# Expert pairs on one core: scatter products of 64 rows for each column half, the pass branch of VectorE ahead of the last pair, and repeated products on TensorE inside the last pair

## The chip, the core and the metric

The kernel runs on one core of a Trainium2 chip. The core has a matrix engine (PE, TensorE), a vector engine (DVE), a scalar engine (ACT), GpSimd (POOL) and a queue engine (SP), which here only issues transfers. Each engine has an instruction stream of its own, and they wait for each other through semaphores. The metric is the device time of one execution in microseconds (us).

## The reference, cut to what matters

A two-layer encoder on 256 tokens of width 1024, all in float32. Each layer has a dense part (convolution, attention, cross attention) and then a mixture of 32 experts, of which each token uses two. The change lies in the expert part.

```
def hier_moe(u, w_group, b_group, w_router, b_router, w1, w3, w2):
    ...
    weights = g_w * jax.nn.softmax(top_v, axis=-1)
    expert = (g_sel * EXPERTS_PER_GROUP + top_i).astype(jnp.int32)
    y = grouped_swiglu(xf, expert, w1, w3, w2)
    out = jnp.einsum('nkd,nk->nd', y, weights.astype(y.dtype))
    return out.reshape(B, S, D)

def expert_block(args):              # inside grouped_swiglu
    xb, e = args
    hdn = jax.nn.silu(xb @ w1[e]) * (xb @ w3[e])
    return hdn @ w2[e]

def reference(...):
    for i in range(DEPTH):           # DEPTH = 2
        ...
        h = h + hier_moe(rmsnorm(h, norm_ffn_g[i]), ...)
    return rmsnorm(h, final_norm_g)
```

## The kernel before, in words

The 32 experts of a layer are worked through as 16 pairs. A pass gives each expert up to 32 tokens (CAP); if some expert has more, all pairs are gone through again, which these inputs do not ask for. For one pair PE runs these steps, each in a function of its own:

- `gather`: multiplies the token rows by a 0/1 selection (`sel`, made by DVE), so that the tokens of the pair's two experts lie side by side.
- `up_product` (L2132): tokens times w1 and w3 of both experts. For each of 8 chunks there are four products, 32 columns of the array each, so the four share the array. Its first half waits for the semaphores of the first halves of the weights, its second half for those of the second halves.
- `turn_up` (L2150): four transposes of the result, once ACT has copied it out of PSUM (L1102). ACT then takes silu (L1106) and DVE multiplies (L1612).
- `down_product` (L2161): the hidden columns times w2. Its four products give, for expert e and column half h of the output, 32 rows of PSUM bank 3 at block 2e + h.
- `turn_spread` (L2113): transposes `spread`, the selection times the router's weight (DVE, L1597), written twice (`dup`) so that each of the four 32-row blocks has a copy. ACT copies it out as `scat` in two versions (L1087, L1088), one with the rows of column half 1 zeroed by a mask column of the constants, one with those of half 0 zeroed.
- `scatter` (L2173): after DVE has copied bank 3 to `y_sb` (L1616), four products of 128 rows (two token halves s, two column halves) add the pair's result to the residual rows, which stand in PSUM banks 4 to 7. After each s it raises the semaphore `added[s]`.

SP brings in the weights, 12.6 MB a pair, into slots that PE frees through the semaphore `freed`. The slabs of the last pair of a layer come in halves. In layer 0 the first slabs of layer 1's dense part (w_xkv, then w_in) are queued behind them.

Around the last pair: PE, DVE, ACT and SP each run the middle pairs in a loop. PE then loads the number of passes from SBUF (L2216), branches (L2217) over a block that holds all pairs once more, and does `last_pair` behind it (L2200). DVE does the last two pairs' part (`pair_tail`) behind its loop, and only then loads the number and branches (L1652, L1653). After the last layer ACT squares the summed rows (L1127), DVE scales them (L1673 to L1678) and SP stores them. After layer 0 the next dense part begins: ACT splits landed weights in a high part (L819) and DVE in a low part (L1213), DVE splits the memory operand (L1278), and PE runs its products high (L1753, L1754) and low (L1758).

The order of all work on an engine is the order in which the code is written. `again` (L2081 on) repeats a product of two constants into a PSUM bank that nobody reads; the kernel before calls it around the router.

## Time and profile before

| | us |
|---|---|
| median of 3 timed runs | 1727.71 |
| lowest and highest of them | 1727.01, 1729.36 |
| the profiled execution | 1730.33 |
| its span in the trace | 1728.5 |
| PE busy, share of the span | 1485.5, 86% |
| DVE busy | 616.5, 36% |
| ACT busy | 521.4, 30% |
| mean granted PE clock, of full speed | 0.928 |

The profile is of one execution. Busy shares are averages over parts with different limits: in the dense parts PE is busy without a gap and the transfer engines are partly idle, in the expert parts it is the other way round. A row of the timeline gives the start in us from the span's start, the duration in us, the engine, the source line, the operation, the tiles, and the count; brackets give the idle time before it and what ended it. "PEldq" and "DVEq" are the sequencers of PE and DVE, which run registers, loads and branches.

### The profile page before, as it was taken

To read this page: it belongs to the slowest core of one execution; us is meant where nothing else is said; L and a number is where in the kernel's file an instruction comes from. 1 tells how busy PE (TensorE), PEld (TensorE's weight loads), DVE (VectorE), ACT (ScalarE), POOL (GpSimd) and SP (SyncE) were. 2 spreads that over 40 slices of the span, in tenths; PEclk is the share of its full clock that TensorE was granted. 3 is DMA by queue.
4 is the path that set the end of the run, shared out by engine and by line. 5 is a ranking of instruction groups with operands and counts; after the bars stand their busy time and mean duration, and the time that the engine had idled before them with its cause. 6 is when DMAs were issued, how large, how long until landed. Compare 5 with 4: busy or idle time off the path is not lost.

```text
span 1728.5 us, 23513 instructions
## 1 busy us (share of the span) xinstructions
PE 1485.5 (86%) x9704; PEld 992.7 (57%) x9704; DVE 616.5 (36%) x1020; ACT 521.4 (30%) x825; POOL 49.5 (3%) x96
## 2 busy tenths in 40 slices
PE   8999999999976767676799999999999676867676
PEld 7879889897432323232277888998864232323222
DVE  5557786654110000001064668775531000000101
ACT  5535655553100000000163465635431000000001
POOL 3011000000000000000000200000000000000000
PEclk8999999999998888888899999999999888888888
DMA  8536344766999999999964462357579999999997
GB/s 236 195 122 212 106 147 162 276 243 266 385 426 428 429 427 428 428 428 429 418 220 169 129 206 99 136 206 286 201 304 429 427 428 428 429 427 430 428 426 289
DMA packets 92832, 531.08 MB, mean 307 GB/s; under 512 B 5992, under 2 KB 6184, under 8 KB 66118
## 3 DMA queue, kind: packets, MB, share of 16 engines
q1 hardware_dynamic: 89600, 524.12, 75.6%
q0 software_dynamic: 3136, 5.73, 1.6%
q8 instruction: 61, 1.00, 0.2%
q14 instruction: 23, 0.19, 0.0%
q10 hardware_dynamic: 12, 0.05, 0.0%
HBM read 524.63 MB, written 1.05 MB: 304 GB/s over the span
## 4 chain that ended last, share of the span: by engine, by line
PE 65%; DMA 30%; DVE 2%; ACT 2%; issue 1%; PEldq 0%; DVEq 0%; SPq 0%; ACTq 0%
DMA ring<-in_w_dram 28%; PE ps L2132 16%; PE ps L1753 7%; PE ps L1758 7%; PE ps L1754 7%; PE ps L1809 4%; PE ps L1810 4%; PE ps L1815 4%; PE ps L2104 2%; DMA ring<-in_w_xkv_dram 2%; PE ps L1855 2%; PE ps L2161 2%; PE ps L1778 1%; PE ps L1784 1%; PE ps L1779 1%; PE ps L2173 1%
## 5 line engine op out<-in xcount | busy, mean ns | idle before, releaser
L2132 PE MATMUL ps<-ring,work 128*32 128x512 f32 x1440 | 282.4, 720 | 190.1 <-DMA ring<-in_w_dram 182.5
L1213 DVE TENSOR_TENSOR weight_split<-ring,weight_split 128x1024 fp32r<-128x1024 f32 x224 | 270.7, 1222 | 163.4 <-ACT weight_split L819 161.3
L819 ACT ACTIVATE weight_split<-ring 128x1024 fp32r<-128x1024 f32 x224 | 234.2, 1058 | 216.0 <-PE ps L1815 86.0
L2132 PEld LDWEIGHTS ps<-ring,work 128*32 128x32 f32 x1440 | 69.2, 130 | 389.7 <-DMA ring<-in_w_dram 203.3
L1612 DVE TENSOR_TENSOR work<-tail,ps 128x256 f32<-128x256 f32 x32 | 13.5, 421 | 661.2 <-ACT tail L1106 661.2
L1753 PE MATMUL ps<-operand_split,weight_split 128*128 128x256 f32 x896 | 227.7, 292 | 1.2 <-PE ps L1758 0.6
L1754 PE MATMUL ps<-operand_split,weight_split 128*128 128x256 f32 x896 | 219.5, 282 | 0.0
L2132 PE MATMUL ps<-big,work 128*32 128x512 f32 x576 | 192.6, 705 | 1.1 <-DVE work L1604 1.1
L1753 PEld LDWEIGHTS ps<-operand_split,weight_split 128*128 128x128 f32 x896 | 171.0, 191 | 15.0 <-issue 12.9
L1754 PEld LDWEIGHTS ps<-operand_split,weight_split 128*128 128x128 f32 x896 | 171.3, 191 | 2.0 <-issue 1.9
L1102 ACT ACTIVATE tail<-ps 128x512 f32<-128x512 f32 x32 | 33.7, 1054 | 443.7 <-PE ps L2132 443.7
L2104 PEld LDWEIGHTS ps<-work,big 128*128 128x128 f32 x1024 | 119.1, 192 | 38.4 <-issue 37.0
L2104 PE MATMUL ps<-work,big 128*128 128x64 f32 x1024 | 124.2, 275 | 9.9 <-PE ps L2132 9.9
L1758 PE MATMUL ps<-operand_split,weight_split 128*128 128x256 f32 x896 | 125.8, 283 | 0.6 <-DVE weight_split L1213 0.6
L2173 PE MATMUL ps<-sqo,tail 128*128 128x512 f32 x256 | 118.4, 605 | 3.2 <-DVE sqo L1616 1.6
L1758 PEld LDWEIGHTS ps<-operand_split,weight_split 128*128 128x128 f32 x896 | 115.6, 192 | 0.8 <-DVE weight_split L1213 0.8
L1809 PE MATMUL ps<-weight_split,operand_split 128*128 128x512 f32 x288 | 114.4, 397 | 0.0
L1810 PE MATMUL ps<-weight_split,operand_split 128*128 128x512 f32 x288 | 113.3, 393 | 0.0
L1087 ACT ACTIVATE tail<-ps,cst 128x256 f32<-128x256 f32 x32 | 15.2, 474 | 301.2 <-PE ps L2173 287.1
L2161 PE MATMUL ps<-ring,work 128*32 128x512 f32 x544 | 81.8, 602 | 0.0
L2173 PEld LDWEIGHTS ps<-sqo,tail 128*128 128x128 f32 x256 | 46.0, 189 | 58.1 <-issue 45.9
L1815 PE MATMUL ps<-weight_split,operand_split 128*128 128x512 f32 x288 | 77.8, 392 | 0.0
(253 smaller groups left out, 1692.5 us busy)
## 6 DMA issues: line engine op xcount, KB each, us to landing
ring<-in_w_dram SPq DMA_DIRECT2D x118, 2048.0 KB, 28.4
big<-in_w_dram SPq DMA_DIRECT2D x56, 2048.0 KB, 27.2
ring<-in_w_in_dram SPq DMA_DIRECT2D x28, 2048.0 KB, 8.0
big<-in_w_dram SPq DMA_DIRECT2D x20, 1024.0 KB, 18.8
ring<-in_w_xkv_dram SPq DMA_DIRECT2D x8, 2048.0 KB, 8.1
ring<-in_w_dram SPq DMA_DIRECT2D x12, 1024.0 KB, 22.4
ring<-in_w_attn_out_dram SPq DMA_DIRECT2D x4, 2048.0 KB, 7.9
ring<-in_w_conv_out_dram SPq DMA_DIRECT2D x4, 2048.0 KB, 8.4
```

The costliest lines, as they stand in the source:

```text
L819: act.activation(split_quarter(k, 0), landed_quarter(k), ACT.Copy).then_inc(w_hi, 1)
L1213: dve.tensor_tensor(split_quarter(k, 1), landed_quarter(k), split_quarter(k, 0).bitcast(F32), ALU.subtract).then_inc(w_lo, 1)
L1753: pe.matmul(dst, hi[:, k, :], xs[0][:, k, :], start=(k == 0), stop=False)
L1754: pe.matmul(dst, hi[:, k, :], xs[1][:, k, :], start=False, stop=False)
L1758: last = pe.matmul(dst, lo[:, k, :], xs[0][:, k, :], start=False, stop=(k == DC - 1))
L1809: pe.matmul(dst[s], xh, hi[:, k, :], start=(c == 0 and k == 0), stop=False)
L1810: pe.matmul(dst[s], xl, hi[:, k, :], start=False, stop=False)
L1815: last = pe.matmul(dst[s], xs[0][:, 2 * c + k, s * P:(s + 1) * P], lo[:, k, :], start=False, stop=False)
L2104: last = pe.matmul(ps[:, 0, c * 2 * CAP:(c + 1) * 2 * CAP], uN[:, s, c * P:(c + 1) * P], sel[:, s].rearrange("p e s -> p (e s)"), start=(s ...
L2132: last = pe.matmul(ps[CAP * j:CAP * (j + 1), 1, :], xe[:, k, e * CAP:(e + 1) * CAP], up_slot(slots[j])[:, k, :], start=(k == 0), stop=(k = ...
L2161: last = pe.matmul(ps[CAP * j:CAP * (j + 1), 3, :], up_t[:, f, e, :], down_slot(slots[4 + e])[:, f, half * SLAB:(half + 1) * SLAB], start= ...
L2173: last = pe.matmul(ps[:, 4 + 2 * s + half, :], scat[:, half, s * P:(s + 1) * P], y_sb, start=False, stop=True, skip_group_check=True)
```

## The change

Four things are changed.

1. Scatter. `down_product` puts expert e and column half h at block 2h + e, so that one column half fills 64 neighbouring rows. `spread` is laid out to match. ACT makes one plain copy `scat` in place of two masked ones, and each of the four scatter products takes the 64 rows of its column half in place of 128 rows half of which are zero. The mask constants go, and `scat` has half its size.
2. DVE. The load of the number of passes and the branch stand ahead of the last pair's `pair_tail` in place of behind it.
3. PE, last pair only. `up_product` calls `again(5, 0)` behind its wait for the tokens and ahead of its wait for the weights.
4. PE, last pair only. `again(1, 0)` stands between `up_product` and `turn_up`, and again between `turn_up` and `down_product`.

```
...
-C_MLO = C_SIGN + 1
-C_MHI = C_MLO + 1
-C_LAM = C_MHI + 1
+C_LAM = C_SIGN + 1
...
+WARM_UP = 5
...
-    c[:, C_MLO] = (p // CAP) % 2 == 0
-    c[:, C_MHI] = (p // CAP) % 2 == 1
...
-        tail = sb("tail", [P, 2 * T + SLAB + FC * 2 * CAP])
+        tail = sb("tail", [P, T + SLAB + FC * 2 * CAP])
...
-        scat = rt(2, T)
+        scat = rt(T)
...
                 def scatter_columns(n):
                     act.wait_ge(gt_done, n + 1)
-                    act.activation(scat[:, 0, :], ps[:, 2, 0:T], ACT.Copy, scale=cst[:, C_MLO:C_MLO + 1])
-                    act.activation(scat[:, 1, :], ps[:, 2, 0:T], ACT.Copy,
-                                   scale=cst[:, C_MHI:C_MHI + 1]).then_inc(scat_ready, 1)
+                    act.activation(scat, ps[:, 2, 0:T], ACT.Copy).then_inc(scat_ready, 1)
                 def next_scatter_columns():
...
                     if again:
                         dve.wait_ge(gt_done, n)
                     for dup in range(2):
-                        dve.tensor_tensor(spread[:, :, :, dup, :], sel,
+                        dve.tensor_tensor(spread[:, :, dup, :, :], sel,
                                           two(tok_w, i).unsqueeze(3).to_broadcast([P, TT, 2, CAP]),
                                           ALU.mult).then_inc(spread_ready, 1)
...
                 with dve.Fori(0, PAIRS - 2) as i:
                     pair_two_on(i)
                 pair_tail(dve.snap(u))
-                pair_tail(dve.snap(u), more=False)
                 passes = dve.value_load(npass_i[0:1, 0:1], min_val=1, max_val=MAX_PASSES)
                 with dve.If(passes > 1):
                     with dve.Fori(1, passes) as _p:
+                        pair_tail(dve.snap(u), more=False)
                         dve.drain()
                         dve.tensor_scalar(rank, rank, -float(CAP), None, ALU.add)
                         dve.drain()
...
                         with dve.Fori(0, PAIRS - 2) as i:
                             pair_two_on(i)
                         pair_tail(dve.snap(u))
-                        pair_tail(dve.snap(u), more=False)
                     dve.nop()
-                dve.nop()
+                pair_tail(dve.snap(u), more=False)
             fc = Chain(dve, fin_ch)
             dve.wait_ge(fin_g, 16)
...
                     pe.wait_ge(spread_ready, n * 2 + 2)
                     for s in range(TT):
                         last = pe.transpose(ps[:, 2, s * P:(s + 1) * P],
-                                            spread[:, s].rearrange("p e w s -> p (e w s)"), ident)
+                                            spread[:, s].rearrange("p w e s -> p (w e s)"), ident)
                     last.then_inc(gt_done, 1)
                 def first_tokens():
...
                     gather(n, 1)
                     turn_spread(n)
-                def up_product(n, slots, landed):
+                def up_product(n, slots, landed, more):
                     pe.wait_ge(xe_ready, n + 1)
+                    if not more:
+                        again(WARM_UP, 0)
                     for k in range(DC):
                         if k % (DC // 2) == 0:
                             pe.wait_ge(*landed[k // (DC // 2)])
...
                             pe.wait_ge(*landed[f // 2])
                         for j in range(4):
                             e, half = j // 2, j % 2
-                            last = pe.matmul(ps[CAP * j:CAP * (j + 1), 3, :], up_t[:, f, e, :],
+                            g = 2 * half + e
+                            last = pe.matmul(ps[CAP * g:CAP * (g + 1), 3, :], up_t[:, f, e, :],
                                              down_slot(slots[4 + e])[:, f, half * SLAB:(half + 1) * SLAB], start=(f == 0),
                                              stop=(f == FC - 1), skip_group_check=True)
                     last.then_inc(y_done, 1)
...
                     pe.wait_ge(y_out, n + 1)
                     for s in range(TT):
                         for half in range(HALVES):
-                            last = pe.matmul(ps[:, 4 + 2 * s + half, :], scat[:, half, s * P:(s + 1) * P], y_sb,
+                            at = slice(2 * CAP * half, 2 * CAP * (half + 1))
+                            last = pe.matmul(ps[:, 4 + 2 * s + half, :], scat[at, s * P:(s + 1) * P], y_sb[at, :],
                                              start=False, stop=True, skip_group_check=True)
                         last.then_inc(added[s], 1)
                     pe.reg_add(u, u, 1)
...
                 def pair(slots, ups, downs, more=True):
                     n = pe.snap(u)
-                    up_product(n, slots, ups)
+                    up_product(n, slots, ups, more)
                     if more:
                         gather(n + 1, 0)
+                    else:
+                        again(1, 0)
                     turn_up(n)
                     if more:
                         gather(n + 1, 1)
+                    else:
+                        again(1, 0)
                     down_product(n, slots, downs)
                     if more:
                         turn_spread(n + 1)
```

PE at the end of the program, from the last pair's first row on, before. `ring` and `big` are weight slots, `work` the tokens, `cst` the constants, `tail` the copied result:

```order
L2200 ISA
L2129 ISA [waits moe_tokens_ready]
L2132 MATMUL ps<-ring,work 32x512 [waits last_up_halves_0_landed]
...
L2150 MATMUL ps<-cst,tail 128x128 [waits moe_up_done,moe_scatter_ready,moe_up_out]
L2150 MATMUL ps<-cst,tail 128x128 x3
L2158 ISA [waits moe_hidden_ready]
L2161 MATMUL ps<-big,work 32x512 [waits last_down_halves_0_landed]
```

The same place now:

```order
L2202 ISA
L2078 MATMUL ps<-cst 128x512 [waits moe_tokens_ready]
L2078 MATMUL ps<-cst 128x512 x4
L2125 ISA
L2128 MATMUL ps<-ring,work 32x512 [waits last_up_halves_0_landed]
...
L2078 MATMUL ps<-cst 128x512 [waits moe_up_done]
L2146 MATMUL ps<-cst,tail 128x128 [waits moe_scatter_ready,moe_up_out]
L2146 MATMUL ps<-cst,tail 128x128 x3
L2078 MATMUL ps<-cst 128x512
L2154 ISA [waits moe_hidden_ready]
L2158 MATMUL ps<-big,work 32x512 [waits last_down_halves_0_landed]
```

Five products of 512 columns stand between the branch and the last pair's first weight product, and one before and one behind the transposes; all stand behind the branch.

DVE at the end of the program, before, from the end of the block that is branched over:

```order
L1612 TENSOR_TENSOR work<-tail,ps 128x256 [waits moe_silu_ready]
L1616 COPY sqo<-ps 128x512 [waits moe_down_done]
L1617 ISA
L1654 COMPARE_AND_BRANCH
L1653 UNCONDITIONAL_BRANCH
L1673 TENSOR_SCALAR small<-small 128x1 [waits final_squares,final_gain_in]
```

And now:

```order
L1612 ISA
L1648 COMPARE_AND_BRANCH
L1647 UNCONDITIONAL_BRANCH
L1660 ISA
L1607 TENSOR_TENSOR work<-tail,ps 128x256 [waits moe_silu_ready]
L1611 COPY sqo<-ps 128x512 [waits moe_down_done]
L1667 TENSOR_SCALAR small<-small 128x1 [waits final_squares,final_gain_in]
```

The last pair's multiply and copy have moved behind the branch; what follows them is the next work without a branch between.

## Rows read from the trace of the kernel before

**Rows 1.** Busy time of a stretch: length, PE, PEld, DVE, ACT, POOL; granted clock, DMA share, GB/s.

```profile
480.00:830.00 350.00, 250.66 (x1680) 105.53 (x1680) 29.92 (x72) 27.33 (x48) 0.00 (x0) 0.85 1.01 428
```

**Rows 2.** The chain that ended last, layer 1's last pair: start us, us, what.

```profile
1699.91 10.07 PE ps L2132 x64
...
1712.76 5.34 PE ps L2161 x32
...
1718.87 2.00 PE ps L2173 x4
```

**Rows 3.** PE's sequencer by line: ns min/median/max, first and last start us.

```profile
L2216 PEldq TENSOR_LOAD <-npass_i x2: 314/403/492, 842.3 to 1692.8; - x2
...
L2217 PEldq COMPARE_BRANCH  x2: 6152/6164/6176, 843.2 to 1693.5; - x2
```

**Rows 4.** The same for the branches of PE's loop and of DVE's pass branch.

```profile
L2211 PEldq COMPARE_BRANCH  x8: 76/213/252, 576.9 to 1692.7; - x8
...
L1653 DVEq COMPARE_BRANCH  x2: 56/62/67, 867.5 to 1718.9; - x2
```

**Rows 5.** Transfers in 846 to 848 us, the instruction queue: packets, MB, share.

```profile
q8 instruction: 1, 0.02, 3.4%
```

**Rows 6.** Timeline of SP: issues of layer 1's last pair, two of them.

```profile
1680.38 0.80 SPq L568 DMA_DIRECT2D ring<-in_w_dram  x2
...
1683.81 0.33 SPq L568 DMA_DIRECT2D ring<-in_w_dram  x1
```

**Rows 7.** Issue to landing, us at the end: first issued at 1680.38, then at 1683.81.

```profile
ring<-in_w_dram SPq DMA_DIRECT2D x1, 1024.0 KB, 14.0
...
ring<-in_w_dram SPq DMA_DIRECT2D x1, 1024.0 KB, 20.4
```

**Rows 8.** Timeline of PE around layer 0's last pair.

```profile
842.08 3.70 PE L2173 MATMUL ps<-sqo,tail 128*128 128x512 f32 x8
849.65 1.05 PE L2132 MATMUL ps<-ring,work 128*32 128x512 f32 x1 [3.88 <-issue]
...
861.24 0.62 PE L2161 MATMUL ps<-big,work 128*32 128x512 f32 x2 [1.00 <-DVE work L1612]
...
864.56 0.62 PE L2161 MATMUL ps<-big,work 128*32 128x512 f32 x2 [1.40 <-DMA ring<-in_w_dram]
...
867.30 3.70 PE L2173 MATMUL ps<-sqo,tail 128*128 128x512 f32 x8 [0.81 <-DVE sqo L1616]
871.08 0.38 PE L1753 MATMUL ps<-operand_split,weight_split 128*128 128x256 f32 x1
```

**Rows 9.** Stretches of both last pairs, columns as in rows 1.

```profile
849.65:852.50 2.85, 2.85 (x16) 0.81 (x20) 0.00 (x0) 0.00 (x0) 0.00 (x0) 0.50 1.03 428
...
1699.91:1705.90 5.99, 5.99 (x30) 1.44 (x34) 0.00 (x0) 0.00 (x0) 0.00 (x0) 0.50 1.00 414
...
1712.76:1716.10 3.34, 3.34 (x16) 0.81 (x20) 0.00 (x0) 0.92 (x2) 0.00 (x0) 0.50 0.08 32
```

**Rows 10.** Pieces of the chain in layer 1 at the full clock.

```profile
1276.60 1.72 PE ps L2084 x4
...
1296.24 3.62 PE ps L2161 x32
...
1304.33 7.05 PE ps L2132 x64
```

**Rows 11.** Timeline of ACT behind layer 0's last pair.

```profile
869.97 2.01 ACT L819 ACTIVATE weight_split<-ring 128x1024 fp32r<-128x1024 f32 x2 [4.61 <-DMA ring<-in_w_xkv_dram]
```

**Rows 12.** Timeline of DVE behind layer 0's last pair.

```profile
867.76 3.25 DVE L1278 SCALAR_TENSOR_TENSOR operand_split<-memT,pk,operand_split 128x256 fp32r<-128x256 f32 x8 [0.52 <-issue]
871.06 1.23 DVE L1213 TENSOR_TENSOR weight_split<-ring,weight_split 128x1024 fp32r<-128x1024 f32 x1
```

**Rows 13.** The chain that ended last, behind layer 0: PE's first low products.

```profile
873.25 0.96 PE ps L1758 x8
```

**Rows 14.** Groups by line, 871 to 1260 us, PE: busy, mean ns, idle before.

```profile
L1753 PE MATMUL ps<-operand_split,weight_split 128*128 128x256 f32 x448 | 113.4, 291 | 0.4 <-PE ps L1758 0.3
```

More of the change, by code:

```diff
@@ L59 @@
 C_SIGN = C_INVF + 1
-C_MLO = C_SIGN + 1
-C_MHI = C_MLO + 1
-C_LAM = C_MHI + 1
+C_LAM = C_SIGN + 1
 C_OML = C_LAM + LAYERS
@@ L97 @@
 UPS = 2 * UP_HALF
+WARM_UP = 5
 PER_PAIR = UPS + 4
@@ L235, in constants @@
     c[:, C_INVF] = np.exp(step * (p % HALF).astype(np.float32) / np.float32(HALF))
-    c[:, C_MLO] = (p // CAP) % 2 == 0
-    c[:, C_MHI] = (p // CAP) % 2 == 1
     for i in range(LAYERS):
@@ L271, in encoder @@
         sqo = sb("sqo", [P, ATTN_STEPS // 4, P])
-        tail = sb("tail", [P, 2 * T + SLAB + FC * 2 * CAP])
+        tail = sb("tail", [P, T + SLAB + FC * 2 * CAP])
         ps = ctx.enter_context(nc.psum_tensor("ps", [P, 8, SLAB], F32))
@@ L407, in encoder @@
         roff[0] = 0
-        scat = rt(2, T)
+        scat = rt(T)
         up_sb = rt(SLAB)
@@ L1086, in scatter_columns @@
                     act.wait_ge(gt_done, n + 1)
-                    act.activation(scat[:, 0, :], ps[:, 2, 0:T], ACT.Copy, scale=cst[:, C_MLO:C_MLO + 1])
-                    act.activation(scat[:, 1, :], ps[:, 2, 0:T], ACT.Copy,
-                                   scale=cst[:, C_MHI:C_MHI + 1]).then_inc(scat_ready, 1)
+                    act.activation(scat, ps[:, 2, 0:T], ACT.Copy).then_inc(scat_ready, 1)
                 def next_scatter_columns():
@@ L1596, in pair_spread @@
                     for dup in range(2):
-                        dve.tensor_tensor(spread[:, :, :, dup, :], sel,
+                        dve.tensor_tensor(spread[:, :, dup, :, :], sel,
                                           two(tok_w, i).unsqueeze(3).to_broadcast([P, TT, 2, CAP]),
@@ L1650, in _ @@
                 pair_tail(dve.snap(u))
-                pair_tail(dve.snap(u), more=False)
                 passes = dve.value_load(npass_i[0:1, 0:1], min_val=1, max_val=MAX_PASSES)
@@ L1654, in _ @@
                     with dve.Fori(1, passes) as _p:
+                        pair_tail(dve.snap(u), more=False)
                         dve.drain()
@@ L1663, in _ @@
                         pair_tail(dve.snap(u))
-                        pair_tail(dve.snap(u), more=False)
                     dve.nop()
-                dve.nop()
+                pair_tail(dve.snap(u), more=False)
             fc = Chain(dve, fin_ch)
@@ L2113, in turn_spread @@
                         last = pe.transpose(ps[:, 2, s * P:(s + 1) * P],
-                                            spread[:, s].rearrange("p e w s -> p (e w s)"), ident)
+                                            spread[:, s].rearrange("p w e s -> p (w e s)"), ident)
                     last.then_inc(gt_done, 1)
@@ L2122, in first_tokens, with up_product @@
                     turn_spread(n)
-                def up_product(n, slots, landed):
+                def up_product(n, slots, landed, more):
                     pe.wait_ge(xe_ready, n + 1)
+                    if not more:
+                        again(WARM_UP, 0)
                     for k in range(DC):
@@ L2160, in down_product @@
                             e, half = j // 2, j % 2
-                            last = pe.matmul(ps[CAP * j:CAP * (j + 1), 3, :], up_t[:, f, e, :],
+                            g = 2 * half + e
+                            last = pe.matmul(ps[CAP * g:CAP * (g + 1), 3, :], up_t[:, f, e, :],
                                              down_slot(slots[4 + e])[:, f, half * SLAB:(half + 1) * SLAB], start=(f == 0),
@@ L2172, in scatter @@
                         for half in range(HALVES):
-                            last = pe.matmul(ps[:, 4 + 2 * s + half, :], scat[:, half, s * P:(s + 1) * P], y_sb,
+                            at = slice(2 * CAP * half, 2 * CAP * (half + 1))
+                            last = pe.matmul(ps[:, 4 + 2 * s + half, :], scat[at, s * P:(s + 1) * P], y_sb[at, :],
                                              start=False, stop=True, skip_group_check=True)
@@ L2180, in pair @@
                     n = pe.snap(u)
-                    up_product(n, slots, ups)
+                    up_product(n, slots, ups, more)
                     if more:
                         gather(n + 1, 0)
+                    else:
+                        again(1, 0)
                     turn_up(n)
@@ L2186, in pair @@
                         gather(n + 1, 1)
+                    else:
+                        again(1, 0)
                     down_product(n, slots, downs)
```

## The prediction

> **What bounds the kernel now.** I read the stretches first. From 480 to 830 us, inside layer 0's expert part, the transfer engines are full (428 GB/s, share 1.01) while PE is busy for 250.66 of 350 us [rows 1]: each pair waits for its weights. Whatever PE, DVE or ACT save in those pairs is therefore saved in idle time. This goes for the shorter scatter of pairs 0 to 14, for the one ACT copy in place of two, and for the `spread` layout; I cost all three at nothing, and the cover is those 99 us of idle PE time, about 8 us a pair.
>
> So the change can only show where the transfers run out: at the last pair of each layer. There I read the chain of waits. In layer 1 the last pair's up product begins at 1699.91 and takes 10.07, the down product begins at 1712.76 and takes 5.34, the scatter begins at 1718.87, and its first half is over after 2.00 [rows 2]. Layer 0 is read from the timeline: up product at 849.65, down product at 861.24 with a wait for a transfer until 864.56, scatter at 867.30 [rows 8].
>
> **Why PE waits before the last pair.** The change treats this wait as one that may be filled, so what ends it decides. PE idles 3.88 us before 849.65, and the profile names no releaser ("issue") [rows 8]. The weights are not it: the last of the first halves is issued at 1680.38 and lands 14.0 us later, at 1694.4, 5.5 us before PE begins [rows 6, 7]. What fits is PE's own sequencer: it loads the number of passes at 842.3 and 1692.8, begins the branch at 843.2 and 1693.5, and this branch takes 6.15 and 6.18 us, so it ends at 849.4 and 1699.7, when the product begins [rows 3]. A loop branch on the same sequencer takes at most 0.25 us, DVE's pass branch at most 0.07 [rows 4]. One packet of the instruction queue moves between 846 and 848 [rows 5], so I read the stall as a fetch of the code branched to. All added products stand behind this branch, so they begin where the wait ends.
>
> The Trainium skill ("Runtime: NRT & Kernel Launch", Instruction fetch mechanics) says that a taken branch whose target is outside of the pages at hand has to fetch them before it can go on. The rows agree: 6.16 us and one instruction packet. By that rule the stall does not depend on what PE still computes, which speaks against the first rival below.
>
> **The change part by part.** The sum is made against the profiled execution (1730.33, span 1728.5), which is 2.6 above the median of 1727.71; I then add the difference to the median.
>
> *Five repeated products.* Four records of a repeated product, two products, take 1.72 at the full clock, so one is 0.86 and five are 4.28 [rows 10]. After the stall the clock is low, at 0.50 of full, which is the 1.2 of its two levels of 1.2 and 2.4 GHz: from 849.65 for 2.85 us in layer 0, and from 1699.91 for 5.99 us in layer 1 [rows 9]. A low clock costs half of its duration, now as before; only other work is done in it. So the up product ends 4.28 later than now in layer 1. In layer 0 it ended at 861.24 less the chain of 2.77 between the two products, at 858.47. Now: 849.65 + 4.28 + 7.05 at full clock [rows 10] + half of 2.85 = 862.4, 3.9 later.
>
> *One product on either side of the transposes.* 0.86 each. From the end of the up product to the down product 2.77 us pass (1712.76 less 1709.98 in layer 1) [rows 2], of which the transposes take some 0.6, the rest being waits for ACT and DVE; before the down product PE idles 1.00 [rows 8]. Both fit at full clock and cost nothing; at the low clock (1.7 each) each would add some 0.7. I take nothing, as the five products ahead have by then raised the clock.
>
> *Down product.* In layer 1 it takes 5.34 because the clock fell once more, to 0.50 from 1712.76 to 1716.1, after PE had stood idle for most of the 2.8 us before [rows 2, 9]; at full clock it takes 3.62 [rows 10]. With PE fed in between, I expect the fall to go: 1.7 saved. In layer 0 it had not fallen. So the timed runs may have had this loss or not, and the saving in them is 0 to 1.7.
>
> *Scatter.* Eight records take 3.70 [rows 8]. No product on 64 rows is in the trace. The nearest row is the up product: four tiles of 32 columns share the array, so 64 records take 7.05, 0.44 for each four [rows 10]. If two tiles of 64 rows share it likewise, the scatter takes half: 1.9. If not, 3.70 as now. I take 1.9, by the column tiles. At the end of the program this is worth 0.9: the first square starts that much sooner, and ACT does the second one only behind the first one's root, so the rest moves along.
>
> *DVE's branch.* In layer 0 DVE pauses 0.52 between its copy and L1278 [rows 12]. Ahead of the last pair DVE has no work during the whole up product (10.07 in layer 1 [rows 2]); that hides the branch, and 0.5 goes from DVE behind layer 0. In layer 1 DVE waits for ACT's square at that point, so nothing is gained.
>
> *Layer 1's end, summed:* + 4.28 - 0.9 - (1.7 or 0) = + 1.7 or + 3.4.
>
> *Layer 0's end.* Here the transfer at 864.56 hides work today, and behind the pair PE waits for ACT's first split, whose slab lands at 869.97 [rows 11]. Now the down product begins at 862.4 + 2.77 = 865.2, has its weights, and ends at 868.8 instead of 866.5. DVE copies 0.69, then does its eight L1278 in 3.25 and the first L1213 in 1.23 [rows 12]: 868.8 + 0.7 + 0.1 + 3.25 + 1.23 = 874.1, against 872.3 today. PE's scatter ends at 871.5, its high products (1.9 us) at 873.4, and it then has to wait for that L1213. Its first low products stood at about 873.0 to 873.1 in the trace (873.25 in the chain [rows 13]) and now start at 874.15: + 1.1. In the dense part that follows PE has next to no gap (the 448 products of L1753 found it idle for 0.4 us in all [rows 14]), so this stays. Had the low clock lasted 5.99 instead of 2.85, as in layer 1, it would be + 2.6. The transfers at 864.56 hid that difference before; they no longer do.
>
> *Together:* 1.7 + 1.1 = + 2.8 at the least, 3.4 + 2.6 = + 6.0 at the most. The one layer shows the short low clock, the other the long one, so I take the middle: + 4.3, that is 1727.7 + 4.3 = 1732.0.
>
> **The rivals.** *First, the other side: the stall hangs on the scatter.* The fetched packet moves about 1 us behind the end of the scatter of pair 14 (842.08 + 3.70 = 845.8), and in both layers that distance is alike. If the branch is held until PE has drained, the scatter's 1.8 us come off the start of the last pair. Then layer 1 gives -0.1 to + 1.6 and layer 0, which falls back under the cover of the transfers, 0 to + 0.8: together -0.1 to + 2.4, around 1728.8. Against it: loop branches take 0.25 us at most while the same scatters run [rows 4]. It turns the verdict to "no change" if more than about 1 us of the scatter's gain reaches the start.
>
> *Second, the 64-row products do not share the array.* The scatter stays at 3.70. Layer 1 loses its 0.9; in layer 0 PE is held by its own scatter until 873.3, 2.2 behind today, 3.7 with the long low clock. Together + 4.8 to + 8.0, around 1734.1. The Trainium skill ("TensorEngine Tiling (Array Packing)", Key Properties) says that tiles operate independently and may run in parallel; no product on 64 rows is in this trace.
>
> *Third, the wait is one that can be filled.* If the repeated products ran inside the wait, say because the stall shortens as the code moves by 16 rows, the up product would run at full clock and be held only by the second halves, which land at 1683.81 + 20.4 = 1704.2 [rows 6, 7]. It would end at 1704.2 + 3.5 = 1707.7 instead of 1710.0, and the down product would begin at 1710.5. Its last weights land between 1712.8, as the transfer share is 0.08 from there on, and some 1.4 later [rows 9], so with 1.8 for its second half it ends between 1714.6 and 1716.0 instead of 1718.1. With the scatter's 0.9, and nothing in layer 0, that is -3.0 to -4.4, around 1724.0. Against it: the added code stands behind the branch, and the stall is the same 6.16 in both layers.
>
> **Chances.** A measurement of this kernel can tell about 0.2%, 3.5 us, from no change; that is 1731.2. Forecast 0.61, of which three quarters lie above 1731.2 (its span is 1730.5 to 1733.7). First rival 0.18, all within. Second 0.11, all above. Third 0.07, half of it beyond -3.5. 0.03 for what I don't see. Slower: 0.46 + 0.11 + 0.01 = 0.58. Same: 0.15 + 0.18 + 0.03 + 0.01 = 0.37. Faster: 0.04 + 0.01 = 0.05. The range runs from 1727.8 (leaving out the third rival and the lower half of the first) to 1734.5 (leaving out the upper part of the second).
>
> **What would show it.** In the profile of the changed kernel: PE's pass branch again at about 6.16 us, beginning 1 us after the scatter of pair 14 begins, and ten records of the repeated product behind it, the first at about 849.6; if the branch ends 1.8 sooner relative to that scatter's start, the first rival is right. The eight scatter records in 1.9 or in 3.7. The up product of layer 1 ending near 1714.2, of layer 0 near 862.4. No clock of 0.50 in the down products. In layer 0 the row of the transfer ending PE's wait gone, DVE's first L1213 at about 872.9, and PE's first L1758 about 1.1 to 2.6 later than 873.1. The forecast is wrong if the repeated products begin before the branch ends, or if the branch is far from 6.16 us.

## The result, and the profile after

| | before | changed |
|---|---|---|
| median of 20 runs each, alternating, us | 1727.01 | 1732.2 |
| lowest and highest | 1724.64, 1730.08 | 1728.34, 1735.77 |
| the profiled execution | 1730.33 | 1733.08 |
| its span | 1728.5 | 1731.3 |

The ratio is 1.0026, with a 95% interval of 1.002 to 1.0033: 4.5 us slower, between 3.5 and 5.7; the medians are 5.2 apart. The page of the changed kernel:

```profile
span 1731.3 us, 23538 instructions
...
PE 1439.4 (83%) x9732; PEld 974.7 (56%) x9732; DVE 616.5 (36%) x1020; ACT 506.7 (29%) x793; POOL 49.4 (3%) x96
```

PE is busy for 46 us less than before and ACT for 15 us less, and the kernel is slower. Nearly all of that saving fell in pairs that wait for their weights. The stretch of [rows 1], now:

```profile
480.00:830.00 350.00, 227.45 (x1672) 94.77 (x1674) 29.97 (x72) 20.82 (x35) 0.00 (x0) 0.83 1.01 428
```

Half of PE's saving, 23.2 us, lies in this stretch, and the transfers run at the same 428 GB/s.

PE's pass branch, by line (ns min/median/max, first and last start us):

```profile
L2219 PEldq COMPARE_BRANCH  x2: 6077/6124/6172, 842.8 to 1696.0; - x2
```

The last pair of layer 1 in the chain that ended last (start us, us, what):

```profile
1695.01 1.99 PE ps L2171 x8
1697.00 5.20 issue
1702.20 5.96 PE ps L2078 x10
1708.16 7.05 PE ps L2128 x64
...
1718.00 3.68 PE ps L2158 x32
...
1722.45 1.15 PE ps L2171 x4
```

L2171 is the scatter, L2078 a repeated product, L2128 the up product, L2158 the down product. The scatter's eight records take 1.99, against 3.70 [rows 8], but the "issue" behind it has grown to 5.20. In the chain of the kernel before it was:

```profile
1696.23 3.68 issue
```

The branch begins 1.0 to 1.2 us behind the start of the scatter, as before, and lasts as long as before [rows 3]. One packet of the instruction queue moves 3 to 4 us behind its start, in 1699 to 1700 us, as one did 3 to 5 us behind it before [rows 5]:

```profile
q8 instruction: 1, 0.02, 6.7%
```

Then come the ten records of the five products, and only then the up product. Beside rows 2: the repeated and up products take 13.01 where the up product took 10.07, the down product 3.68 where it took 5.34, and the first half of the last scatter 1.15 where it took 2.00.

Layer 0, PE's timeline:

```profile
849.10 7.54 PE L2078 MATMUL ps<-cst 128*128 128x512 f32 x10 [5.50 <-issue]
...
863.82 1.10 PE L2078 MATMUL ps<-cst 128*128 128x512 f32 x2 [0.18 <-PE ps L2128]
864.82 0.66 PE L2146 MATMUL ps<-cst,tail 128*128 128x128 f32 x4
865.31 1.02 PE L2078 MATMUL ps<-cst 128*128 128x512 f32 x2
866.48 0.62 PE L2158 MATMUL ps<-big,work 128*32 128x512 f32 x2
...
870.93 1.99 PE L2171 MATMUL ps<-sqo,tail 64*128 64x512 f32 x8 [0.81 <-DVE sqo L1611]
...
875.23 0.98 PE L1752 MATMUL ps<-operand_split,weight_split 128*128 128x256 f32 x6 [0.21 <-DVE weight_split L1208]
```

The row of a transfer that ended PE's wait at 864.56 [rows 8] has no counterpart: the up product now ends past 863, and the down product starts late with all its weights there. What PE then waits for, at 875.23, is DVE's low part of the first weights. The first low products stood at about 873.1 before (873.25 in the chain [rows 13]). DVE's timeline shows the chain that leads there, and that its branch's pause of 0.52 [rows 12] is gone:

```profile
870.18 0.69 DVE L1611 COPY sqo<-ps 128x512 f32<-128x512 f32 x1 [3.84 <-PE ps L2158]
870.79 3.25 DVE L1273 SCALAR_TENSOR_TENSOR operand_split<-memT,pk,operand_split 128x256 fp32r<-128x256 f32 x8
...
873.96 1.22 DVE L1208 TENSOR_TENSOR weight_split<-ring,weight_split 128x1024 fp32r<-128x1024 f32 x1
```

The mean granted clock, as a share of full speed, in three stretches: the repeated products of layer 0, those of layer 1, and layer 1's down product (columns as in rows 1, the clock third from the end).

```profile
849.10:856.60 7.50, 7.50 (x14) 2.90 (x15) 0.00 (x0) 0.00 (x0) 0.00 (x0) 0.60 1.01 419
...
1702.20:1708.16 5.96, 5.96 (x14) 2.46 (x18) 0.00 (x0) 0.00 (x0) 0.00 (x0) 0.76 1.01 418
...
1718.00:1721.70 3.70, 3.64 (x32) 0.97 (x32) 0.00 (x0) 0.92 (x2) 0.00 (x0) 1.00 0.00 0
```

From the means, at 0.50 and 1.00 of full, the low clock (1.2 GHz) lasted 6.0 us in layer 0 (7.50 x (1 - 0.60) / 0.5) and 2.9 us in layer 1. Before it was 2.85 and 5.99 [rows 9]: the same two lengths, in the other order.

### The profile page after: what moved, and what is told of

Its sections match the earlier page's. It is cut to its first block, busy times and chain, and to the rows that moved or that the text cites. A ratio compares the mean times of both kernels' runs of the same rounds, so it can differ in the third digit from the quotient of the medians.

```text
span 1731.3 us, 23538 instructions
## 1 busy us (share of the span) xinstructions
PE 1439.4 (83%) x9732; PEld 974.7 (56%) x9732; DVE 616.5 (36%) x1020; ACT 506.7 (29%) x793; POOL 49.4 (3%) x96
## 4 chain that ended last, share of the span: by engine, by line
PE 63%; DMA 31%; DVE 3%; ACT 1%; issue 1%; PEldq 0%; SPq 0%; DVEq 0%; ACTq 0%
DMA ring<-in_w_dram 30%; PE ps L2128 15%; PE ps L1747 7%; PE ps L1752 7%; PE ps L1748 7%; PE ps L1803 4%; PE ps L1804 4%; PE ps L1809 4%; PE ps L1849 2%; PE ps L2098 1%; PE ps L1772 1%; PE ps L1778 1%; PE ps L2158 1%; PE ps L1773 1%; PE ps L2078 1%
## 5 line engine op out<-in xcount | busy, mean ns | idle before, releaser
L2128 PE MATMUL ps<-ring,work 128*32 128x512 f32 x1440 | 275.6, 708 | 231.6 <-DMA ring<-in_w_dram 231.6
L1208 DVE TENSOR_TENSOR weight_split<-ring,weight_split 128x1024 fp32r<-128x1024 f32 x224 | 270.4, 1223 | 159.8 <-ACT weight_split L816 157.8
L2128 PEld LDWEIGHTS ps<-ring,work 128*32 128x32 f32 x1440 | 68.1, 128 | 425.5 <-DMA ring<-in_w_dram 253.2
L2128 PE MATMUL ps<-big,work 128*32 128x512 f32 x576 | 187.1, 684 | 1.1 <-DVE work L1599 1.1
L2098 PE MATMUL ps<-work,big 128*128 128x64 f32 x1024 | 124.2, 275 | 10.1 <-PE ps L2128 10.1
L1084 ACT ACTIVATE tail<-ps 128x256 f32<-128x256 f32 x32 | 12.3, 384 | 250.0 <-PE ps L2171 236.0
L2158 PE MATMUL ps<-ring,work 128*32 128x512 f32 x544 | 80.0, 595 | 0.0
L2158 PE MATMUL ps<-big,work 128*32 128x512 f32 x480 | 72.7, 595 | 0.3
L2171 PE MATMUL ps<-sqo,tail 64*128 64x512 f32 x256 | 63.6, 615 | 3.2 <-DVE sqo L1611 1.6
```

What stands on the lines that cost most here:

```text
L1208: dve.tensor_tensor(split_quarter(k, 1), landed_quarter(k), split_quarter(k, 0).bitcast(F32), ALU.subtract).then_inc(w_lo, 1)
L2098: last = pe.matmul(ps[:, 0, c * 2 * CAP:(c + 1) * 2 * CAP], uN[:, s, c * P:(c + 1) * P], sel[:, s].rearrange("p e s -> p (e s)"), start=(s ...
L2128: last = pe.matmul(ps[CAP * j:CAP * (j + 1), 1, :], xe[:, k, e * CAP:(e + 1) * CAP], up_slot(slots[j])[:, k, :], start=(k == 0), stop=(k = ...
L2158: last = pe.matmul(ps[CAP * g:CAP * (g + 1), 3, :], up_t[:, f, e, :], down_slot(slots[4 + e])[:, f, half * SLAB:(half + 1) * SLAB], start= ...
L2171: last = pe.matmul(ps[:, 4 + 2 * s + half, :], scat[at, s * P:(s + 1) * P], y_sb[at, :], start=False, stop=True, skip_group_check=True)
```

## The experiments

The theory: the whole loss is the five repeated products, because they stand behind PE's pass branch and so begin only when it ends. The rivals were those of the prediction; after the first runs the question was what the wait itself costs. Each run has one profile. Runs 1 to 4 shared one chip and one set of runs of the kernel before (median 1727.18), runs 5 to 8 another (1726.82), runs 9 and 10 a third (1726.92). Ratios are against these.

**1. Only the five products, on the kernel before.** (`...` marks what is left out of an edit.)

```
...
-                def up_product(n, slots, landed):
+                def up_product(n, slots, landed, more):
                     pe.wait_ge(xe_ready, n + 1)
+                    if not more:
+                        again(WARM_UP, 0)
```

> The kernel before with the five repeated products alone, everything else as before. My theory (the products begin only when PE's pass branch has ended, with the weights landed, so they push the last pair out): + 4.3 at layer 1's end, less 1.7 if the clock stays up in the down product, and in layer 0 PE's scatter, still 3.70 us long, ends 2.2 to 3.7 later; together + 4.8 to + 8.0 against before. Rival (the wait is one that can be filled, the products run inside it): 0 or below, -3 at best. In the profile: ten records of the repeated product behind the branch, which takes 6.1 to 6.2 us.

Measured: 1733.17, ratio 1.0037 (1.0023 to 1.005), that is 6.4 us slower (4.0 to 8.6). Its chain:

```profile
1695.72 3.70 PE ps L2176 x8
1699.42 3.60 issue
1703.01 6.04 PE ps L2085 x10
1709.06 7.05 PE ps L2135 x64
...
1718.88 5.38 PE ps L2164 x32
```

The 3.60 of idle time is about what it was before (3.68), and the ten records stand behind it. Note the last row: the down product again takes 5.38, at a mean clock of 0.68. So in layer 1 the five products did not keep the clock up across the gap behind the up product; in layer 0 of this profile it stayed at 1.00.

**2. The changed kernel without the five.**

```
                     pe.wait_ge(xe_ready, n + 1)
-                    if not more:
-                        again(WARM_UP, 0)
```

> The changed kernel without the five repeated products; the scatter of 64 rows, DVE's earlier branch and the two single products stay. My theory: all of the loss goes. Layer 1 gains 0.9 from the scatter and 0 to 1.7 from the clock in the down product, layer 0 is covered by its transfers again: -0.9 to -2.6 against before. Rival (the loss comes from another part, from the 64-row scatter or the moved branch): still + 3 or more against before. In the profile: first up product of the last pair at 7.2 to 7.4 us behind the start of the scatter ahead.

Measured: 1725.24, ratio 0.9984 (0.9975 to 0.9993), 2.8 us faster than before (1.2 to 4.3), the lowest ratio of all the kernels here.

```profile
1694.82 1.99 PE ps L2169 x8
...
1702.23 10.01 PE ps L2126 x64
...
1715.03 3.68 PE ps L2156 x32
...
1719.48 1.15 PE ps L2169 x4
```

The up product takes 10.01 as before, while down product and scatter have the short times of the changed kernel. So the other parts of the change are worth 2.8, and the five products cost 7.3 on top of them (1.0026 less 0.9984, times 1727; by the two intervals some 5 to 9).

**3. The single products gone too.**

```
                     if more:
                         gather(n + 1, 0)
-                    else:
-                        again(1, 0)
                     turn_up(n)
                     if more:
                         gather(n + 1, 1)
-                    else:
-                        again(1, 0)
```

> The changed kernel without any repeated product in the last pair. It differs from the run without the five by the two single products alone. My theory: -0.9 against before, with the down product of layer 1 at the low clock in some executions; so 0 to 1.7 slower than the run without the five. Rival (the single products lie on the path and cost 0.1 to 0.2 each in both layers): faster than that run by 0.2 to 0.4.

Measured: 1725.66, ratio 0.9994 (0.9985 to 1.0003). By the ratios this is 1.7 slower than run 2, by the medians 0.4, and the intervals overlap. It fits the expectation without proving it. In its one profile, an execution of 1722.86, layer 1's down product ran at the full clock without any single product (first row, its first half), and its second half was then held by its last weights; layer 0's ran at a mean of 0.69 (second row; columns as in rows 1):

```profile
1706.47:1708.37 1.90, 1.90 (x16) 0.42 (x16) 0.00 (x0) 0.92 (x2) 0.00 (x0) 1.00 0.72 302
858.52:863.70 5.18, 5.18 (x32) 1.18 (x32) 0.00 (x0) 4.11 (x10) 0.00 (x0) 0.69 1.05 388
```

So the fall of the clock ahead of the down product comes in some executions and layers and not in others. Over all profiles, two layers each: without the single products (before and runs 1, 3, 5, 8, 10) 8 of 12 down products ran at a mean clock of 0.67 to 0.70; with them (changed and runs 2, 4, 6, 7, 9) all 12 ran at 1.00.

**4. Ten products in place of five.**

```
-WARM_UP = 5
+WARM_UP = 10
```

> The changed kernel with ten in place of five repeated products. My theory: each product is 0.86 us of PE on the path in both layers, at full clock by then: + 4.3 in layer 1 and + 4.3 in layer 0, where nothing covers them any more, so + 8.6 against the changed kernel and + 12.5 to + 14 against before. Rival (part of the five still lies in a wait, so they cost less than the next five): the difference to the changed kernel is clearly more than twice that kernel's loss plus what the scatter gives back; by the profile the first five cost 4.3 less covers, so the slope tells. Rival (the price is the low clock and not the work): less than + 4 against the changed kernel.

Measured: 1740.33, ratio 1.0083 (1.0069 to 1.0097): 8.1 above the changed kernel by the medians, 9.8 by the ratios. Five more products a layer, ten in all, at 0.86 make 8.6.

```profile
1701.69 10.26 PE ps L2078 x20
1711.95 7.05 PE ps L2128 x64
```

By this slope each further product behind the branch costs its own length. Five had already used up what cover there was, layer 0's transfer at 864.56 [rows 8].

**5. The branch three pairs earlier, on the kernel before.** If the branch's 6 us stall is what costs, it should pay to put it where PE waits for weights anyway.

```
-                with pe.Fori(1, TRIPLES) as _i:
+                with pe.Fori(1, TRIPLES - 1) as _i:
                     for kind in range(KINDS):
                         kind_pair(kind)
...
                 passes = pe.value_load(npass_i[0:1, 0:1], min_val=1, max_val=MAX_PASSES)
                 with pe.If(passes > 1):
...
+                for kind in range(KINDS):
+                    kind_pair(kind)
                 last_pair()
```

> The kernel before with PE's load of the passes and its branch three pairs earlier: the loop runs one round less, and the last round stands behind the branch. Theory (the wait ahead of the last pair is the fetch behind the branch, and the branch can hide where PE waits for weights anyway): the idle time of 3.7 to 3.9 us ahead of the last pair goes, the up product follows the scatter at once and then waits for its second halves, which land at about 1704.2; layer 1 ends 1 to 3 us sooner, layer 0 is held by its transfers at 864.56 as before; together -1 to -3. Rival (the wait is one for weights): the idle time stays and nothing changes. In the profile the branch of 6.2 us lies ahead of pair 12, where PE idles more than 8 us anyway.

Measured: 1728.99, ratio 1.0011 (0.9998 to 1.0023). Not faster; the expectation was wrong. The stall has moved:

```profile
L2217 PEldq COMPARE_BRANCH  x2: 6399/6548/6697, 751.9 to 1603.8; - x2
```

But a wait for the second halves of the weights has taken its place in layer 1:

```profile
1683.36 20.03 DMA ring<-in_w_dram
...
1703.43 6.56 PE ps L2132 x32
...
1712.77 5.31 PE ps L2161 x32
```

PE starts the up product early, stops between its halves until 1703.4, and does the second half in 6.56 at the low clock, where 3.5 was to be had. It ends at 1709.99; before, it ended at 1709.98 [rows 2], in a span of the same 1728.5. In layer 0 its timeline shows such a wait too, of 3.65 us:

```profile
852.46 1.05 PE L2132 MATMUL ps<-ring,work 128*32 128x512 f32 x1 [3.65 <-DMA ring<-in_w_dram]
```

**6. The same on run 2's kernel** (the edit of run 5 without `again(5, 0)`).

> The changed kernel without the five repeated products, and with PE's branch three pairs earlier. Theory: what the run without the five gives and what the earlier branch gives, partly the same microseconds, since the transfers become the bound: -2 to -4.2 against before.

Measured: 1725.59, ratio 0.9996 (0.9987 to 1.0005). The -2 to -4.2 expected did not come, and nothing was gained over run 2 (0.9984).

```profile
1679.31 21.07 DMA ring<-in_w_dram
...
1700.42 5.55 PE ps L2126 x32
```

The second half starts when its transfer lands and runs partly at the low clock.

Moving the branch also tests what the stall is. In run 5 a packet of the instruction queue moves 3 to 5 us behind the start of the branch in both layers, as before and after the change, though the branch stands some 90 us earlier; the kernel before moves no such packet in 749 to 760 or in 1600 to 1615. That fits a fetch of the code branched to. It is no proof: run 5 also moves one between 841 and 850, where PE has no such stall.

**7. Run 6 with the five products between the halves of the up product.** Here the wait is one for data, so it can be filled. (Shown against run 6.)

```
                     for k in range(DC):
+                        if k == DC // 2 and not more:
+                            again(WARM_UP, 0)
                         if k % (DC // 2) == 0:
                             pe.wait_ge(*landed[k // (DC // 2)])
```

> The same with the five repeated products put between the two halves of the last pair's up product, where PE now waits for the second halves. Theory: they lie inside a real wait here (some 6 us in layer 1), cost nothing, and keep the clock up for the second half: -3 to -4.2 against before, 0 to 1.5 faster than the run without them. Rival (repeated products always cost): slower than that run by 2 or more.

Measured: 1726.05, ratio 0.9997 (0.9987 to 1.0006). The same five products that cost some 7 us behind the branch cost nothing that can be told here (0.5 us by the medians against run 6, 0.2 by the ratios, within either interval). PE's timeline of layer 0:

```profile
846.64 4.56 PE L2078 MATMUL ps<-cst 128*128 128x512 f32 x10
...
852.88 0.62 PE L2128 MATMUL ps<-ring,work 128*32 128x512 f32 x1 [1.68 <-DMA ring<-in_w_dram]
```

They run at full clock, and 1.68 us of the wait are left behind them (1.79 in layer 1). But they gain nothing either, and the -3 to -4.2 expected failed: in layer 1 the last transfer of the program now ends the chain.

```profile
1686.22 26.42 DMA ring<-in_w_dram
...
1712.68 1.97 PE ps L2158 x16
```

**8. Only DVE's branch ahead of the last pair, on the kernel before.**

```
                 pair_tail(dve.snap(u))
-                pair_tail(dve.snap(u), more=False)
                 passes = dve.value_load(npass_i[0:1, 0:1], min_val=1, max_val=MAX_PASSES)
...
+                pair_tail(dve.snap(u), more=False)
```

> The kernel before with DVE's load of the passes and its branch ahead of the last pair alone. Theory: 0.5 us go from DVE behind layer 0, where it ends together with ACT's first split, so 0 to -0.1; no difference that can be measured. Rival (DVE was the last to be ready behind layer 0): -0.5.

Measured: 1726.51, ratio 1.0 (0.999 to 1.0011): no difference, as expected.

**9. The five products ahead of the load and the branch** (run 2's kernel, with a wait for the tokens).

```
                 pe.wait_ge(*due(rank_ready, 1))
+                pe.wait_ge(xe_ready, pe.snap(u) + 1)
+                again(WARM_UP, 0)
                 passes = pe.value_load(npass_i[0:1, 0:1], min_val=1, max_val=MAX_PASSES)
```

> The changed kernel with the five repeated products moved ahead of PE's load of the passes and its branch, behind a wait for the last pair's tokens. Theory (PE's engine works on what was issued while its sequencer stalls in the branch): the products run inside the stall, right behind the scatter, and cost nothing; issuing them delays the branch by up to 1 us. The clock stays up for all or most of the last pair's up product in both layers (7 to 8.6 us in place of up to 10.1). Against before: -0.9 by the scatter, -1.7 to 0 by the down product, -1.5 to 0 by the up product, less up to 1 for the delay: -1 to -3. Rival (repeated products cost wherever they stand): + 4 or more.

Measured: 1725.49, ratio 0.9994 (0.9984 to 1.0003), that is -1.0 at the least favourable edge of what was expected, and not resolved from no change. Against run 2 the products cost 1.7 us by the ratios (by the two intervals between nothing and some 4), 0.25 by the medians, where behind the branch they cost 7.3. By line, and then PE's timeline in layer 0:

```profile
L2219 PEldq COMPARE_BRANCH  x2: 5979/6018/6056, 844.3 to 1695.0; - x2
```

```profile
843.04 1.99 PE L2169 MATMUL ps<-sqo,tail 64*128 64x512 f32 x8
844.96 4.56 PE L2078 MATMUL ps<-cst 128*128 128x512 f32 x10
850.56 0.61 PE L2126 MATMUL ps<-ring,work 128*32 128x512 f32 x1 [1.04 <-issue]
```

The branch begins at 844.3, before the repeated products do, and they run inside its stall. PE's idle time falls to 1.04, and the up product starts 7.5 us behind the start of the scatter, as without them (in run 2, 8.0 in layer 0 and 7.4 in layer 1). And the whole up product now has the full clock in layer 0, 7.06 in place of the 8.5 to 10.1 that it takes in the profiles where it comes first behind the branch:

```profile
850.56:857.62 7.06, 7.06 (x64) 2.04 (x64) 0.00 (x0) 0.00 (x0) 0.00 (x0) 1.00 1.01 419
```

So the repeated products do here what they were meant to do, and it pays nothing that can be told. In layer 1 the chain shows what bounds instead:

```profile
1689.19 26.29 DMA ring<-in_w_dram
...
1715.53 1.97 PE ps L2156 x16
```

How near that bound is shows when layer 1's end is measured from one point, the start of pair 14's up product:

| profile | that start | end of span | between |
|---|---|---|---|
| before | 1674.64 | 1728.5 | 53.9 |
| changed | 1677.03 | 1731.3 | 54.3 |
| run 2 | 1677.01 | 1728.3 | 51.3 |
| run 6 | 1670.72 | 1722.0 | 51.3 |
| run 3 | 1670.01 | 1721.1 | 51.1 |
| run 7 | 1673.01 | 1724.3 | 51.3 |
| run 9 | 1675.97 | 1727.1 | 51.1 |

In runs 3, 7 and 9 the last transfer ends PE's wait, 39.5 to 39.6 us behind that start. Run 2 is within 0.2 us of them. By these profiles, once the five products are gone from behind the branch, layer 1 has next to nothing left to win from an earlier branch or a higher clock. That is why runs 6, 7 and 9 gain nothing over run 2.

**10. Only the 64-row scatter, on the kernel before** (with `spread` and `scat` to match; DVE's branch and PE's repeats as before).

```
-                            last = pe.matmul(ps[:, 4 + 2 * s + half, :], scat[:, half, s * P:(s + 1) * P], y_sb,
+                            at = slice(2 * CAP * half, 2 * CAP * (half + 1))
+                            last = pe.matmul(ps[:, 4 + 2 * s + half, :], scat[at, s * P:(s + 1) * P], y_sb[at, :],
```

> The kernel before with the 64-row scatter alone. Theory: the eight records of the scatter take 2.0 in place of 3.7, hidden in 30 of 32 pairs; layer 1's end gains 0.9 (the first half of the scatter is over after 1.15 in place of 2.00), layer 0 nothing: -0.9 against before, that is at the edge of what can be told. Rival (the longer idle time that the shorter scatter leaves in every pair costs clock on the path): 0 or slower.

Measured: 1727.02, ratio 1.0001 (0.9991 to 1.0011). The expected 0.9 lies inside the interval and is not resolved. By line, then the chain:

```profile
L2214 PEldq COMPARE_BRANCH  x2: 5927/5929/5931, 839.9 to 1689.8; - x2
```

```profile
1690.84 5.24 issue
...
1715.05 1.15 PE ps L2170 x4
```

What the scatter saves ahead of the branch comes back as "issue" (5.24 for 3.68), and what it saves at the end shows in the chain as 1.15 for 2.00.

## Why the prediction was right, and where not

The forecast was 1732.0 with a range of 1727.8 to 1734.5, slower; measured were 1732.2 and slower. The main mechanism was right. That the two numbers agree within 0.2 us is luck in part: they set out from different medians of the kernel before (1727.7 and 1727.0), and the two sums below give 2.9 us in the profiles where 4.3 was forecast (the middle of + 2.8 and + 6.0 is 4.4). Point by point:

- **Pairs that wait for weights: right.** Nearly all of the 46 us of PE work and 15 of ACT's went there at no gain, and run 10, which has the scatter's part of it, shows no change (1.0001).
- **What ends PE's wait: right.** The stall is 6.08 to 6.17 with a scatter of half the length, so it does not hang on PE's drain, and the first rival falls. The idle time grew from 3.88 and 3.68 to 5.50 and 5.20. Run 10 has the same without the repeats. The rule cited from the Trainium skill ("Runtime: NRT & Kernel Launch", Instruction fetch mechanics) agrees in that the stall is there in all kernels, from 5.93 to 6.70. It says that execution cannot continue before the fetch; run 9 shows that this holds for the sequencer alone, as PE did 4.56 us of queued products meanwhile. That the 6 us are a fetch remains a reading: an instruction packet goes with the branch when it is moved (run 5), but no run changed the fetch itself.
- **Price of the five products: right in size.** 4.28 a layer was the term (at full clock the ten records took 4.56 in runs 7 and 9, and five more of them 4.3 in run 4); run 1 gave + 6.4 for both layers, within the + 4.8 to + 8.0 expected of it, and run 4 another 8.1 to 9.8 for ten more.
- **64-row products share the array: right.** 1.99 for 3.70; 1.9 was taken. The second rival falls. The sentence of "TensorEngine Tiling (Array Packing)", Key Properties, in the Trainium skill is borne out by this row.
- **The wait cannot be filled: right for these products, wrong as a general reading.** The prediction named their place behind the branch as the evidence against the third rival, and that was the decisive point: runs 7 and 9 put the same five in other places, and there they cost nothing that could be told. The third rival's gain of 3.0 to 4.4 did not come there either (0.5 and 1.0 by the ratios). In their profiles layer 1's stretch is 2.6 to 2.8 shorter than before, but run 2, without the five, has 2.6 of it too: in runs 7 and 9 the down product's second half stood behind the last transfer, 39.6 and 39.5 us behind the start of pair 14's up product, which is 1714.2 in the trace of before and so the latest landing that the prediction allowed.
- **Layer 1's sum: one term was wrong in this profile.** Forecast + 1.7 or + 3.4. In the profile, from the end of DVE's copy for pair 14 to the end of the span it is 36.3 against 36.0: + 0.3. The step that failed is "a low clock costs half of its duration, now as before" with the same duration as before: it lasted 2.9 us and not 5.99, which alone gives back 1.5. It may be no chance: in layer 1 it lasted 2.9 to 3.0 in all three profiles with repeated products behind the branch (changed, runs 1 and 4), and 5.5 to 6.0 in four of the five without (before and runs 2, 8, 10; 2.9 in run 3). With that the up product comes out as measured: + 4.28 - 1.5 = + 2.8, against 13.01 - 10.07 = + 2.9. The down product's - 1.7 and the scatter's - 0.9 came as forecast. That leaves the chain 0.4 longer, and its start came 0.2 sooner: 7.23 from that copy to PE's first record, against 7.42.
- **Layer 0's sum: right, at its upper end.** + 1.1 with the short low clock, + 2.6 with the long one. It was the long one: measured from the start of layer 0's pair 14 scatter, PE's first low products came 2.6 later. They came 2.1 later by the clock of the trace, and that scatter began 0.5 earlier (841.61 by the timeline, 842.08 in [rows 8]). Pair 14's copy in layer 1 came 2.5 later (the chains show it beginning at 1694.27 after and 1691.79 before). The path was the one forecast: down product late, DVE's L1273 and L1208 behind it (L1278 and L1213 before), PE waiting for them, and no slack in the dense part.
- **Why the medians differ by more than the profiles.** The two profiles are 2.8 apart, the medians 5.2 and the ratio 4.5. The 20 runs of one kernel spread over 5.4 and 7.4 us, and the profiled execution stood 3.3 above the median before and 0.9 above it after. One part of the spread is seen above: the low clock behind the stall lasts some 3 or some 6 us, worth 1.5. The short one in layer 0 of the profile before, on which the forecast's lower end rests, was the exception: in the other seven profiles with the branch in that place and nothing ahead of it, it lasted 5.4 to 6.2 there. What decides between the two, and what the rest of the difference is, stays open.
- **What a rest of the change is worth:** the forecast implied - 0.9 to - 2.6 for all but the five products; run 2 gave - 2.8 (- 1.2 to - 4.3). How that splits the medians don't resolve (run 3, without the single products, lies between at 0.9994, run 10 at 1.0001). In the profiles the single products save up to 1.7: layer 1's down product took 3.68 in the changed kernel and in runs 2, 4 and 6, and 5.23 to 5.38 before and in runs 1, 5, 8 and 10, which lack them. Run 3, which lacks them too, kept the clock up in layer 1 and ended as early as run 2 did.

The loss is therefore shown to be the five products behind the branch, by taking them out, adding them alone, doubling them, and moving them. Runs 5 and 6 found no gain from a branch three pairs earlier; that another place could not win back part of the stall is not shown.

## What to carry to other kernels

Before a wait is filled, find what ends it: in this kernel a wait for data took other work at no cost that could be told (run 7), a stall of the engine's own sequencer only such work as was issued ahead of it (run 9); behind it five more products cost their full length (run 4). A wait that is removed uncovers the next one, here the second halves of the weights and then the last transfer, so read when those land before pricing the gain: run 2 already stood within 0.2 us of the last one. Nearly all of the 46 us of PE work saved here lay in a stage that waits for transfers and was worth nothing, while one product of 0.86 us on either side of a gap kept the clock up behind it in all 12 cases profiled, which is worth up to 1.7 where nothing else holds the path.

## What was not expected of the hardware

- The stall of PE's pass branch lasts about the same in all twelve profiles, 5.93 to 6.70 us, in either place and whatever PE computes, while a loop's branch takes 0.25 at most [rows 4]. PE goes on with queued products meanwhile (run 9).
- After the idle time at the branch (3.6 to 6.0 us) the clock stayed low for either 2.9 to 3.0 us or 5.4 to 6.2 us, and both could come in one execution: before, changed and in runs 1, 3 and 4 one layer had the short and the other the long one; in runs 2, 8 and 10 both had the long one.
- After the clock had risen in the up product, some 2.8 us of mostly idle time brought it down once more in 8 of 12 cases (in layer 1 before and in runs 1, 5, 8, 10, in layer 0 in runs 3, 8, 10), and the down product took 5.2 to 5.4; with some 1.0 us of repeated product on either side of the transposes it stayed at 1.00 in 12 of 12.
